# Feed-forward of a hybrid trunk: a seven-product unit in place of the second plain unit, with another order of its blocks

## Chip, cores and metric

The kernel runs on one core of a Trainium2 chip. The metric is the device time of one execution in microseconds (us), lower is better; the time before is the median of three runs, 2020.74 us (2019.19 to 2021.62).

## What is computed

A decoder trunk of four layers on 256 tokens of width 1024, in float32. Each layer is a macaron: half a gated feed-forward, a mixer (stick-breaking attention, Mamba-2 SSD, gated short convolution, attention again), half a gated feed-forward. So there are twelve phases, eight of them feed-forwards, and a last normalization. Only the feed-forward is touched by the change:

```
def rmsnorm(x, g):
    xf = x.astype(jnp.float32)
    y = xf * lax.rsqrt(jnp.mean(xf * xf, axis=-1, keepdims=True) + RMS_EPS)
    return (y * g.astype(jnp.float32)).astype(x.dtype)

def swiglu(x, w_gu, w_down):
    gate, up = jnp.split(x @ w_gu, 2, axis=-1)
    return (jax.nn.silu(gate) * up) @ w_down

for i in range(DEPTH):
    x = x + 0.5 * swiglu(rmsnorm(x, ffn1_norm[i]), ffn1_w_gu[i], ffn1_w_down[i])
    ...
    x = x + 0.5 * swiglu(rmsnorm(x, ffn2_norm[i]), ffn2_w_gu[i], ffn2_w_down[i])
```

`w_gu` is 1024 x 5632 (2816 gate columns, 2816 up columns), `w_down` is 2816 x 1024.

## The kernel before

**Blocks.** Weights stream from HBM in blocks of 128 x 2048 numbers, 1 MB each. A block is loaded by SyncE into one of six slots (three tiles `stage`, three in `arena`), split by ScalarE into a rounded high part `w_hi` (line 734), then by VectorE into the rest `w_lo` (line 1113), and multiplied by TensorE in three passes (high by high, low by high, high by low). `w_hi` and `w_lo` have three buffers each, so ScalarE may split block n only when TensorE has used block n - 3 (`block_used`), VectorE follows ScalarE (`hi_done`), and TensorE waits for VectorE (`lo_done`, `block_in`). A slot is loaded again once VectorE has finished the last split that reads it (`load`).

**Units.** The 2816 hidden columns of a feed-forward are cut into units, numbered 0 to 5 and named by a letter each in `UNITS` (line 51). A P unit has 512 columns in four plain blocks G0, G1, U0, U1 (gate and up, halves of the 1024 rows of `w_gu`). Each is multiplied with both halves of the tokens, 24 matmuls of 128x512. The H unit is half as wide (H0, H1). An S unit has 512 columns too, but cuts tokens, rows and gate/up into halves and takes seven products of half blocks instead of eight, in Strassen's manner: B11, A1, B22, A3, B21, A2, A4, of 12 matmuls each (`product`, line 1735). B blocks are loaded weights, A blocks are sums of them, made in place in the slots: A1 = B12 + B11 and A4 = B21 + the content of A2 are sums by VectorE (`weight_sum`, line 1251). A3 and A2 are made by GpSimd, which adds B22 from HBM onto a slot with an accumulating DMA of 1 MB: onto the slot of A1 once VectorE has finished the sum (line 672), and onto the slot of B11 once the split of A1 is done (line 675).

**After the products.** An S unit's seven results in PSUM are joined by three copies of ScalarE (`part`, line 823), five sums of VectorE (`part_sum`, line 1224) and two products with the silu (`hidden_summed`, line 1220). TensorE then turns the hidden values (`hidden_transpose`, line 1769, eight transposes for a unit of 512 columns), ScalarE and VectorE split them (lines 829, 1230), and the unit's down blocks D0 and D1 (`down`, 24 matmuls each, banks 0 to 3) multiply them with `w_down`. A unit's down blocks come later than the unit: `DOWNS` (line 52) says how many waiting down blocks are placed in each unit's stretch, and `ffn_order` (line 65) writes out the one order `FFN_ORDER` that all engines follow. Before the change it is (unit, block):

```
0G0 0G1 0U0 0U1 1B11 1A1 1B22 0D0 0D1 1A3 1B21 1A2 1A4 2H0 2H1 1D0 3B11 3A1 1D1 3B22 2D0
3A3 3B21 3A2 3A4 4G0 4G1 3D0 4U0 4U1 3D1 5B11 5A1 5B22 4D0 5A3 5B21 5A2 5A4 4D1 5D0 5D1
```

**The order on VectorE and ScalarE.** While TensorE has block i, VectorE first does what block i - 1 released (`released`), then the split of block i + 2, then a sum of weights if one is due. The sum for A1 is due when block i + 2 is a B11, that for A4 when it is a B21. ScalarE does the copies that block i - 1 released, then the split of block i + 2. Before the first block of a unit TensorE waits in `gate_banks_free`; after an S unit that is for its third copy and its third sum of parts, which reads bank 5. The lines are:

```
for i in range(len(FFN_ORDER)):
    if i >= 1:
        released(*FFN_ORDER[i - 1], i - 1)
    ...
        split(b0 + i + 2)
    if i + 2 < len(FFN_ORDER):
        u, name = FFN_ORDER[i + 2]
        if name == "B11":
            weight_sum(u, "A1")
        ...
        elif name == "B21":
            weight_sum(u, "A4")
```

Of the kernel before, what the change touches and what calls it, by code (L numbers as in the profile page):

```python
# [47 lines left out]
SSD_STAGE_SLOTS = 3  # L48


UNITS = "PSHSPS"
DOWNS = (0, 2, 1, 2, 2, 1)


def unit_col(u):

    return sum(256 if kind == "H" else 512 for kind in UNITS[:u])


def down_parts(u):  # L60

    return 1 if UNITS[u] == "H" else 2


def ffn_order():

    order, turned, waiting = [], {}, []
    for u, kind in enumerate(UNITS):
        own = {"P": ("G0", "G1", "U0", "U1"), "H": ("H0", "H1"),
               "S": ("B11", "A1", "B22", "A3", "B21", "A2", "A4")}[kind]  # L70
        own = [(u, name) for name in own]
        lead, head = {"P": (1, 2), "H": (1, 2), "S": (2, 3)}[kind]
        if u:
            waiting += [(u - 1, f"D{j}") for j in range(down_parts(u - 1))]
        now, waiting = waiting[:DOWNS[u]], waiting[DOWNS[u]:]
        order += own[:lead]
        if u:
            turned[u - 1] = len(order) - 1
        if kind == "S" and UNITS[u - 1] == "H":
            order += now[:1]  # L80
            now = now[1:]
        order += own[lead:head]
        if kind == "P":
            order += now[:1] + own[2:] + now[1:]
        else:
            order += now + own[head:]
    turned[u] = len(order) - 1
    return order + waiting + [(u, f"D{j}") for j in range(down_parts(u))], turned


FFN_ORDER, TURNED_AFTER = ffn_order()
N_UNITS, N_SUMS = len(UNITS), UNITS.count("S")
HOME = {"A1": "B11", "A2": "B11", "A3": "B12", "A4": "B21"}
# [13 lines left out]
def build_trunk(nc, x, ffn1_norm, ffn1_w_gu, ffn1_w_down, mix_norm, ffn2_norm, ffn2_w_gu,  # L107
# [98 lines left out]
    def block_columns(n):  # L206

        p = max(q for q in range(n_phases) if base[q] <= n)
        kind, i = PHASES[p][0], n - base[p]
        if kind == "ssd" and i == 1:  # L210
            return KD * SSD_HEADS
        return 4 * 3 * P if kind == "conv" and i < 16 else BLOCK
# [28 lines left out]
    for p, (kind, _, index) in enumerate(PHASES):  # L241
        for i in range(BLOCKS[kind]):
# [4 lines left out]
            u, name = FFN_ORDER[i]  # L247
# [9 lines left out]
    def sums_before(f, u):  # L257

        return N_SUMS * f + UNITS[:u].count("S")

    def hidden_banks_before(f, u):

        return f * sum(down_parts(v) for v in range(N_UNITS)) + sum(down_parts(v) for v in range(u))

    ctx = ExitStack()
    with ctx:
# [839 lines left out]
        def _(dve):  # L1106
            def split(n):

                if n >= total:
                    return  # L1110
                s, q, c = slot_of[n], n % SPLIT_SLOTS, block_columns(n)
                dve.wait_ge(hi_done, n + 1)
                dve.tensor_tensor(w_lo[q][:, 0:c], stage[s][:, 0:c], w_hi[q][:, 0:c].bitcast(F32),  # L1113
                                  ALU.subtract).then_inc(lo_done, 1)
# [93 lines left out]
            def ffn(p):  # L1208
# [24 lines left out]
                def weight_sum(u, name):  # L1233

                    w = lambda b: stage[home[p, u, b][0]][:, :]
                    done = len(SUM_STEP) * sums_before(f, u)
                    if name == "A1":
                        dve.wait_ge(stage_in[home[p, u, "B12"][0]], home[p, u, "B12"][1])
                        to, a, b = w("B11"), w("B12"), w("B11")
                    elif name == "A3":  # L1240
                        dve.wait_ge(stage_in[home[p, u, "B22"][0]], home[p, u, "B22"][1])
                        to, a, b = w("B12"), w("B22"), w("B12")
                    elif name == "A2":
                        to, a, b = w("B11"), w("B22"), w("B11")
                    else:
                        if BY_DMA:
                            dve.wait_ge(a2_in, 16 * (sums_before(f, u) + 1))
                        else:
                            dve.wait_ge(w_summed, done + SUM_STEP["A2"])
                        to, a, b = w("B21"), w("B21"), w("B11")  # L1250
                    dve.tensor_tensor(to, a, b, ALU.add).then_inc(w_summed, 1)

                def x_sums():
                    for i, (a, b, op) in enumerate(((xg[:, 1, :], xg[:, 3, :], ALU.subtract),
                                                    (x_sum[:, 0, :], xg[:, 0, :], ALU.subtract),
                                                    (xg[:, 0, :], xg[:, 1, :], ALU.subtract),
                                                    (xg[:, 2, :], x_sum[:, 1, :], ALU.add))):
                        if i in (1, 3):
                            dve.wait_ge(x_summed, 4 * f + i)
                        dve.tensor_tensor(x_sum[:, i, :], a, b, op).then_inc(x_summed, 1)  # L1260

                def x_sums_lo():
                    for i in range(4):
                        dve.wait_ge(xs_hi_done, 4 * f + i + 1)
                        hi, lo = sum_pair(i)
                        dve.tensor_tensor(lo, x_sum[:, i, :].rearrange("p (k t) -> p k t", k=4), hi.bitcast(F32),
                                          ALU.subtract).then_inc(xs_lo_done, 1)

                def released(u, name, i):

                    if name == "U1":
                        hidden(u, i, 512, lambda h: bank[6 + h][:, :])
                    elif name == "H1":
                        hidden(u, i, 256, lambda h: bank[4 + h][:, 256:512])
                    elif name == "A3":
                        dve.wait_ge(block_used, b0 + i + 1)
                        part_sum(u, p57, p5, bank[6][:, :], 2, ALU.subtract)
                    elif name == "B21":
                        dve.wait_ge(block_used, b0 + i + 1)
                        part_sum(u, hid[:, 0, :], bank[7][:, :], p1, 1, ALU.add)  # L1280
                    elif name == "A2":
                        part_sum(u, sg[:, 0, :], bank[5][:, :], p16, 3, ALU.subtract)
                        dve.wait_ge(part_summed, 5 * sums_before(f, u) + 1)
                        part_sum(u, sg[:, 1, :], p57, p16, 3, ALU.subtract)
                    elif name == "A4":
                        dve.wait_ge(block_used, b0 + i + 1)
                        part_sum(u, hid[:, 1, :], bank[6][:, :], p16, 3, ALU.add)
                        hidden_summed(u, 0)
                        hidden_summed(u, 1)
                        if u == N_UNITS - 1:  # L1290
                            split(b0 + i + 2)
                    for v in range(N_UNITS):
                        if TURNED_AFTER[v] == i:
                            hidden_lo(v)
                    if name == "A1" and not BY_DMA:
                        weight_sum(u, "A3")
# [4 lines that stand above are left out]
                    if i == 1 and N_SUMS:  # L1301
                        x_sums()
                    if i + 2 <= len(FFN_ORDER) and (i == 0 or FFN_ORDER[i - 1] != (N_UNITS - 1, "A2")):
                        split(b0 + i + 2)
                    if i + 2 < len(FFN_ORDER):
                        u, name = FFN_ORDER[i + 2]
                        if name == "B11":
                            weight_sum(u, "A1")
                        elif name == "A3" and not BY_DMA:
                            weight_sum(u, "A2")  # L1310
                        elif name == "B21":
                            weight_sum(u, "A4")
                    if i == 2 and N_SUMS:
                        x_sums_lo()
# [893 lines left out]
```

## Time and profile before

| | value |
|---|---|
| median of three runs | 2020.74 us |
| profiled execution, its own time | 2019.88 us |
| its span, first to last instruction | 2018.0 us |
| PE (TensorE matmul) busy | 1998.2 us, 99% |
| DVE (VectorE) busy | 1566.5 us, 78% |
| ACT (ScalarE) busy | 1187.3 us, 59% |
| POOL (GpSimd) busy | 168.7 us, 8% |
| granted TensorE clock | 1.00 throughout |
| moved by DMA | 419.87 MB, 208 GB/s in the mean |

PE is matmuls, PEld the loads of its stationary operand, which run beside them. A matmul's duration overlaps the next one's, so what it costs is the distance from start to start. The same holds for short overlaps of 0.08 us on DVE. One feed-forward, the fourth phase, lasts from 500.17 us to 678.97 us of the span: 178.80 us.

### The profile page before, as it was taken

To read this page: it belongs to the slowest core of one execution; us is meant where nothing else is said; L and a number is where in the kernel's file an instruction comes from. 1 tells how busy PE (TensorE), PEld (TensorE's weight loads), DVE (VectorE), ACT (ScalarE), POOL (GpSimd) and SP (SyncE) were. 2 spreads that over 40 slices of the span, in tenths; PEclk is the share of its full clock that TensorE was granted. 3 is DMA by queue.
4 is the path that set the end of the run, shared out by engine and by line. 5 is a ranking of instruction groups with operands and counts; after the bars stand their busy time and mean duration, and the time that the engine had idled before them with its cause. 6 is when DMAs were issued, how large, how long until landed. Compare 5 with 4: busy or idle time off the path is not lost.

```text
span 2018.0 us, 25283 instructions
## 1 busy us (share of the span) xinstructions
PE 1998.2 (99%) x10299; PEld 1705.1 (84%) x10299; DVE 1566.5 (78%) x1489; ACT 1187.3 (59%) x1269; POOL 168.7 (8%) x165
## 2 busy tenths in 40 slices
PE   7999999999999999999999999999999999999998
PEld 6888998888888899988888888988888888998887
DVE  6778567778886889968878878778878778568777
ACT  6546576556655676646556555446556556576555
POOL 2000001000000014410001000000001001001000
PEclk9999999999999999999999999999999999999999
DMA  8867535867787484368876867658876867535864
GB/s 275 257 226 229 184 105 138 252 235 229 232 248 210 139 274 132 126 229 239 242 217 194 245 241 193 206 189 248 248 219 188 253 222 232 178 105 142 256 229 114
DMA packets 242183, 419.87 MB, mean 208 GB/s; under 512 B 10668, under 2 KB 92932, under 8 KB 241556
## 3 DMA queue, kind: packets, MB, share of 16 engines
q1 hardware_dynamic: 215732, 363.34, 53.0%
q0 software_dynamic: 26048, 54.61, 15.0%
q8 instruction: 82, 1.34, 0.3%
q10 hardware_dynamic: 288, 0.31, 0.0%
q14 instruction: 33, 0.27, 0.0%
HBM read 417.14 MB, written 1.08 MB: 207 GB/s over the span
## 4 chain that ended last, share of the span: by engine, by line
PE 87%; DVE 7%; ACT 3%; issue 1%; DMA 1%; ACTq 0%; SPq 0%; POOLq 0%; POOL 0%; DVEq 0%
PE bank L1594 51%; PE bank L1735 23%; PE bank L1600 7%; DVE w_lo L1113 3%; PE bank L1769 2%; DVE arena L1461 2%; ACT w_hi L734 2%; PE bank L1627 1%; PE bank L1909 1%; PE bank L1940 1%; DMA stage<-in_ssd_w_in 0%; PE bank L1922 0%; ACT arena L1009 0%; DMA arena<-seg_rows 0%; DMA arena<-in_ffn_norm 0%
## 5 line engine op out<-in xcount | busy, mean ns | idle before, releaser
L1113 DVE TENSOR_TENSOR w_lo<-stage,w_hi 128x2048 fp32r<-128x2048 f32 (+1 forms) x224 | 514.8, 2300 | 152.4 <-ACT w_hi L734 151.2
L1113 DVE TENSOR_TENSOR w_lo<-arena,w_hi 128x2048 fp32r<-128x2048 f32 (+1 forms) x196 | 444.3, 2268 | 162.4 <-ACT w_hi L734 161.7
L734 ACT ACTIVATE w_hi<-stage 128x2048 fp32r<-128x2048 f32 (+1 forms) x224 | 423.3, 1892 | 207.5 <-PE bank L1594 141.7
L734 ACT ACTIVATE w_hi<-arena 128x2048 fp32r<-128x2048 f32 (+1 forms) x196 | 371.7, 1897 | 236.8 <-PE bank L1594 157.0
L1594 PE MATMUL bank<-w_hi,mt_hi 128*128 128x512 f32 x928 | 367.3, 396 | 0.4 <-DVE mt_lo L1347 0.4
L1594 PE MATMUL bank<-w_lo,mt_hi 128*128 128x512 f32 x928 | 361.5, 390 | 0.0
L1594 PE MATMUL bank<-w_hi,mt_lo 128*128 128x512 f32 x928 | 361.0, 390 | 0.0
L1594 PE MATMUL bank<-w_hi,xt_hi 128*128 128x512 f32 x704 | 279.2, 398 | 3.0 <-DVE w_lo L1113 1.3
L1594 PE MATMUL bank<-w_lo,xt_hi 128*128 128x512 f32 x704 | 274.8, 391 | 0.0
L1594 PE MATMUL bank<-w_hi,xt_lo 128*128 128x512 f32 x704 | 251.9, 390 | 0.0
L1594 PEld LDWEIGHTS bank<-w_hi,mt_lo 128*128 128x128 f32 x928 | 174.1, 188 | 37.0
L1600 PE MATMUL bank<-xt_hi,w_hi 128*128 128x256 f32 x704 | 203.4, 290 | 1.2 <-DVE arena L1461 0.7
L1594 PEld LDWEIGHTS bank<-w_hi,mt_hi 128*128 128x128 f32 x928 | 174.3, 188 | 35.1 <-DVE mt_lo L1347 0.8
L1594 PEld LDWEIGHTS bank<-w_lo,mt_hi 128*128 128x128 f32 x928 | 174.5, 188 | 34.5
L1600 PE MATMUL bank<-xt_hi,w_lo 128*128 128x256 f32 x704 | 198.1, 283 | 0.0
L1600 PE MATMUL bank<-xt_lo,w_hi 128*128 128x256 f32 x704 | 195.4, 283 | 0.0
L1594 PEld LDWEIGHTS bank<-w_hi,xt_hi 128*128 128x128 f32 x704 | 133.0, 189 | 33.9 <-issue 3.9
L1594 PEld LDWEIGHTS bank<-w_hi,xt_lo 128*128 128x128 f32 x704 | 132.0, 188 | 27.9
L1594 PEld LDWEIGHTS bank<-w_lo,xt_hi 128*128 128x128 f32 x704 | 133.0, 189 | 26.3
L1735 PE MATMUL bank<-w_hi,mt_hi 128*128 128x512 f32 x384 | 151.0, 393 | 0.1
L1735 PE MATMUL bank<-w_hi,mt_lo 128*128 128x512 f32 x384 | 149.7, 390 | 0.0
L1735 PE MATMUL bank<-w_lo,mt_hi 128*128 128x512 f32 x384 | 149.5, 389 | 0.0
(219 smaller groups left out, 2810.8 us busy)
## 6 DMA issues: line engine op xcount, KB each, us to landing
arena<-in_ffn_w_gu SPq DMA_DIRECT2D x81, 1024.0 KB, 5.3
stage<-in_ffn_w_gu SPq DMA_DIRECT2D x79, 1024.0 KB, 5.3
stage<-in_ffn_w_down SPq DMA_DIRECT2D x96, 512.0 KB, 5.0
arena<-in_ffn_w_down SPq DMA_DIRECT2D x80, 512.0 KB, 4.9
arena<-in_ffn_w_gu POOLq DMA_DIRECT2D x29, 1024.0 KB, 9.6
stage<-in_ffn_w_gu POOLq DMA_DIRECT2D x19, 1024.0 KB, 9.8
stage<-in_ffn_w_gu SPq DMA_DIRECT2D x18, 512.0 KB, 8.7
stage<-in_sb_w_qkv SPq DMA_DIRECT2D x16, 512.0 KB, 4.6
```

The lines of the kernel that those rows point to most:

```text
L734: act.activation(w_hi[q][:, 0:c], stage[s][:, 0:c], ACT.Copy).then_inc(hi_done, 1)
L1113: dve.tensor_tensor(w_lo[q][:, 0:c], stage[s][:, 0:c], w_hi[q][:, 0:c].bitcast(F32), ALU.subtract).then_inc(lo_done, 1)
L1461: dve.scalar_tensor_tensor(chan[:, c, i:SEQ], bank[c][:, 0:SEQ - i], par[:, t:t + 1], chan[:, c, i:SEQ], ALU.mult, ALU.add).then_inc(tap_d ...
L1594: mm = pe.matmul(out_, x_[a], w[b], start=start and (a, b) == (0, 0), stop=stop and (a, b) == (1, 0))
L1600: mm = pe.matmul(out_, w[b], x_[a], start=start and (a, b) == (0, 0), stop=stop and (a, b) == (1, 0), skip_group_check=True)
L1627: mm = pe.transpose(tb[i % 2][:, k * P:(k + 1) * P], xk, ident[:, :])
L1735: mm = pe.matmul(out_[:, :], x[a], w[b], start=start and k == 0 and (a, b) == (0, 0), stop=stop and k == 3 and (a, b) == (1, 0), skip_grou ...
L1769: mm = pe.transpose(tb[b][:, c * SEQ + h * P:c * SEQ + (h + 1) * P], hid[:, h, col:col + P], ident[:, :])
L1909: pe.matmul(z[:, 0:SEQ], kk[:, 0:P], qq, start=True, stop=True, skip_group_check=True)
L1940: pe.matmul(o[:, 0:SEQ], v(0), w[:, 0:SEQ], start=h % 2 == 0, stop=True, skip_group_check=True)
```

## The change

The letters of unit 4 become S, and three units of seven products stand behind each other (3, 4, 5). Where an S unit follows an S unit, the first down block that is placed there goes between its first product B11 and its second one A1, and VectorE's sum for A1 is due one block later (when block i + 1 is B11, not i + 2). `DOWNS` places the down blocks otherwise.

```
--- before
+++ after
@@
-UNITS = "PSHSPS"
-DOWNS = (0, 2, 1, 2, 2, 1)
+UNITS = "PSHSSS"
+DOWNS = (0, 1, 1, 2, 2, 2)
@@
+def adjacent(u):
+
+    return u > 0 and UNITS[u - 1:u + 1] == "SS"
@@ def ffn_order():
         now, waiting = waiting[:DOWNS[u]], waiting[DOWNS[u]:]
-        order += own[:lead]
+        if adjacent(u):
+            order += own[:1] + now[:1]
+            order += own[1:lead]
+            now = now[1:]
+        else:
+            order += own[:lead]
@@ VectorE, ffn(p)
+                    if i + 1 < len(FFN_ORDER):
+                        u, name = FFN_ORDER[i + 1]
+                        if name == "B11" and adjacent(u):
+                            weight_sum(u, "A1")
                     if i + 2 < len(FFN_ORDER):
                         u, name = FFN_ORDER[i + 2]
-                        if name == "B11":
+                        if name == "B11" and not adjacent(u):
                             weight_sum(u, "A1")
```

The order is now, 45 blocks in place of 42:

```
0G0 0G1 0U0 0U1 1B11 1A1 1B22 0D0 1A3 1B21 1A2 1A4 2H0 2H1 0D1 3B11 3A1 1D0 3B22 1D1
3A3 3B21 3A2 3A4 4B11 2D0 4A1 4B22 3D0 4A3 4B21 4A2 4A4 5B11 3D1 5A1 5B22 4D0 5A3 5B21 5A2 5A4 4D1 5D0 5D1
```

What moves on VectorE where unit 3 ends and unit 4 begins, in the first feed-forward. `w_lo` rows are splits, the rows arena<-...bank are sums of parts, 128x2048 rows with no `w_lo` are sums of weights; the number of a `stage` or `arena` slot differs between phases. Before:

```order
L1113 TENSOR_TENSOR w_lo0<-stage2,w_hi0 128x2048 [waits hi_done]
L1224 TENSOR_TENSOR arena<-bank7,arena 128x512 [waits part_copied,block_used]
L1113 TENSOR_TENSOR w_lo1<-arena,w_hi1 128x2048 [waits hi_done]
L1224 TENSOR_TENSOR arena<-bank5,arena 128x512 [waits part_copied]
L1224 TENSOR_TENSOR arena<-arena 128x512 [waits part_copied,part_summed]
L1113 TENSOR_TENSOR w_lo2<-stage0,w_hi2 128x2048 [waits hi_done]
L1224 TENSOR_TENSOR arena<-bank6,arena 128x512 [waits part_copied,block_used]
L1220 TENSOR_TENSOR arena<-arena 128x512 [waits part_summed,silu_done] x2
L1113 TENSOR_TENSOR w_lo0<-stage1,w_hi0 128x2048 [waits hi_done]
```

The four splits are those of 3A4, 4G0, 4G1 and 3D0. After:

```order
L1123 TENSOR_TENSOR w_lo2<-stage1,w_hi2 128x2048 [waits hi_done]
L1234 TENSOR_TENSOR arena<-bank7,arena 128x512 [waits part_copied,block_used]
L1123 TENSOR_TENSOR w_lo0<-stage2,w_hi0 128x2048 [waits hi_done]
L1234 TENSOR_TENSOR arena<-bank5,arena 128x512 [waits part_copied]
L1234 TENSOR_TENSOR arena<-arena 128x512 [waits part_copied,part_summed]
L1123 TENSOR_TENSOR w_lo1<-stage0,w_hi1 128x2048 [waits hi_done]
L1261 TENSOR_TENSOR stage2<-arena,stage2 128x2048 [waits stage_in3]
L1234 TENSOR_TENSOR arena<-bank6,arena 128x512 [waits part_copied,block_used]
L1230 TENSOR_TENSOR arena<-arena 128x512 [waits part_summed,silu_done] x2
L1123 TENSOR_TENSOR w_lo2<-stage2,w_hi2 128x2048 [waits hi_done]
```

The splits are now those of 3A4, 4B11, 2D0 and 4A1, and between that of 2D0 and the last sums of unit 3 stands the sum for 4A1, whose result the next split (of 4A1) reads. The same rows come again where unit 4 ends and unit 5 begins, with 3D1 in the place of 2D0.

On GpSimd, the accumulating transfers of the first feed-forward, before:

```order
L672 DMA arena<-in_ffn_w_gu 128x4x512 [waits w_summed]
L675 DMA arena<-in_ffn_w_gu 128x4x512 [waits lo_done]
L672 DMA arena<-in_ffn_w_gu 128x4x512 [waits w_summed]
L675 DMA arena<-in_ffn_w_gu 128x4x512 [waits lo_done]
L672 DMA stage<-in_ffn_w_gu 128x4x512 [waits w_summed]
L675 DMA arena<-in_ffn_w_gu 128x4x512 [waits lo_done]
```

and after:

```order
L682 DMA arena<-in_ffn_w_gu 128x4x512 [waits w_summed]
L685 DMA arena<-in_ffn_w_gu 128x4x512 [waits lo_done]
L682 DMA arena<-in_ffn_w_gu 128x4x512 [waits w_summed]
L685 DMA arena<-in_ffn_w_gu 128x4x512 [waits lo_done]
L682 DMA arena<-in_ffn_w_gu 128x4x512 [waits w_summed]
L685 DMA stage<-in_ffn_w_gu 128x4x512 [waits lo_done]
L682 DMA arena<-in_ffn_w_gu 128x4x512 [waits w_summed]
L685 DMA stage<-in_ffn_w_gu 128x4x512 [waits lo_done]
```

There are eight in place of six, two for each S unit.

## Rows read from the trace of the kernel before

**Rows 1.** The page: engines' busy time, and the chain that ended last.

```profile
PE 1998.2 (99%) x10299; PEld 1705.1 (84%) x10299; DVE 1566.5 (78%) x1489; ACT 1187.3 (59%) x1269; POOL 168.7 (8%) x165
...
PE 87%; DVE 7%; ACT 3%; issue 1%; DMA 1%; ACTq 0%; SPq 0%; POOLq 0%; POOL 0%; DVEq 0%
```

**Rows 2.** Timeline of PE: start us, us, what; starts of 3A3, 4G0, its turn, 4G1, 3D0.

```profile
590.37 0.39 PE L1735 MATMUL bank<-w_hi,mt_hi 128*128 128x512 f32 x1
...
601.25 0.44 PE L1594 MATMUL bank<-w_hi,xt_hi 128*128 128x512 f32 x1
...
606.75 1.04 PE L1769 MATMUL bank<-ident,arena 128*128 128x128 f32 x8
607.54 0.48 PE L1594 MATMUL bank<-w_hi,xt_hi 128*128 128x512 f32 x1
...
613.11 0.39 PE L1594 MATMUL bank<-w_hi,mt_hi 128*128 128x512 f32 x1
```

**Rows 3.** Timeline of DVE from 3A3 to the end of unit 3, [idle before <-releaser].

```profile
592.58 2.29 DVE L1113 TENSOR_TENSOR w_lo<-arena,w_hi 128x2048 fp32r<-128x2048 f32 x1 [0.94 <-ACT w_hi L734]
594.79 0.68 DVE L1224 TENSOR_TENSOR arena<-arena,bank 128x512 f32<-128x512 f32 x1
595.38 2.29 DVE L1113 TENSOR_TENSOR w_lo<-stage,w_hi 128x2048 fp32r<-128x2048 f32 x1
...
598.19 2.28 DVE L1113 TENSOR_TENSOR w_lo<-stage,w_hi 128x2048 fp32r<-128x2048 f32 x1
600.39 0.68 DVE L1224 TENSOR_TENSOR arena<-bank,arena 128x512 f32<-128x512 f32 x1
600.99 0.68 DVE L1224 TENSOR_TENSOR arena<-arena 128x512 f32<-128x512 f32 x1
601.59 2.28 DVE L1113 TENSOR_TENSOR w_lo<-stage,w_hi 128x2048 fp32r<-128x2048 f32 x1
603.79 0.68 DVE L1224 TENSOR_TENSOR arena<-bank,arena 128x512 f32<-128x512 f32 x1
604.39 1.28 DVE L1220 TENSOR_TENSOR arena<-arena 128x512 f32<-128x512 f32 x2
605.59 2.28 DVE L1113 TENSOR_TENSOR w_lo<-arena,w_hi 128x2048 fp32r<-128x2048 f32 x1
```

**Rows 4.** Timeline of ACT: the split that starts as 3A3 does.

```profile
590.63 1.92 ACT L734 ACTIVATE w_hi<-arena 128x2048 fp32r<-128x2048 f32 x1 [3.52 <-PE bank L1594]
```

**Rows 5.** Timeline around a weight sum: who starts when it ends, and the second transfer.

```profile
517.25 2.29 DVE L1251 TENSOR_TENSOR arena<-arena 128x2048 f32<-128x2048 f32 x1
519.45 2.49 DVE L1266 TENSOR_TENSOR mt_lo<-arena,mt_hi 128x512 fp32r<-128x512 f32 x4
519.57 1.92 ACT L734 ACTIVATE w_hi<-arena 128x2048 fp32r<-128x2048 f32 x1 [2.48 <-DVE arena L1251]
519.83 1.34 POOL L672 DMA_DIRECT2D arena<-in_ffn_w_gu  x1 [14.19 <-DVE arena L1251]
521.86 2.29 DVE L1113 TENSOR_TENSOR w_lo<-arena,w_hi 128x2048 fp32r<-128x2048 f32 x1
...
524.45 1.27 POOL L675 DMA_DIRECT2D arena<-in_ffn_w_gu  x1 [3.27 <-DVE w_lo L1113]
```

**Rows 6.** Timeline at the one place where PE waited for a split.

```profile
19.59 2.28 DVE L1113 TENSOR_TENSOR w_lo<-stage,w_hi 128x2048 fp32r<-128x2048 f32 x1
...
21.93 0.50 PE L1594 MATMUL bank<-w_hi,xt_hi 128*128 128x512 f32 x1 [1.28 <-DVE w_lo L1113]
...
22.26 0.40 PE L1594 MATMUL bank<-w_lo,xt_hi 128*128 128x512 f32 x1
22.26 0.19 PEld L1594 LDWEIGHTS bank<-w_hi,xt_hi 128*128 128x128 f32 x1
22.50 0.40 PE L1594 MATMUL bank<-w_hi,xt_hi 128*128 128x512 f32 x1
```

**Rows 7.** Timeline of PE: starts of 1A1 and of 0D0, with 1A1, turn, 1B22 between.

```profile
525.25 0.39 PE L1735 MATMUL bank<-w_hi,mt_hi 128*128 128x512 f32 x1
...
531.74 0.39 PE L1594 MATMUL bank<-w_hi,mt_hi 128*128 128x512 f32 x1
```

**Rows 8.** Landing times of GpSimd's transfers, line 672 and then line 675.

```profile
DMA to landing us min/median/max: 8.5/8.7/10.1
...
DMA to landing us min/median/max: 9.6/10.5/12.2
```

**Rows 9.** DMA queues from 515 to 540 us, where two accumulating transfers run.

```profile
q0 software_dynamic: 1056, 2.10, 47.8%
```

## The prediction

> **What bounds the kernel now.** I read the page first: TensorE's matmuls are busy 99% of the span and the chain that ended last is 87% PE, so a matmul saved is time saved only as long as nothing else begins to hold TensorE up [rows 1]. Then I read the timeline of one feed-forward. The four products 3A3 to 3A4 take from 590.37 to 601.25 us, 10.88 us or 2.72 us a product of 12 matmuls, with no gap [rows 2]; a plain or down block of 24 matmuls is two of those, 5.44 us. Then I asked how near the others are to holding TensorE up. In a run of products a new split is due every 2.72 us, VectorE's split costs 2.21 us from start to start (592.58 to 594.79) and a sum of parts after it 0.60 us [rows 3]: together 2.81 us, more than a product lasts. So VectorE falls behind by a little with each product there and recovers under down blocks. The reader should see in [rows 3] that only the first row has idle time ahead of it: from 592.58 to 607.87 us VectorE doesn't stop, and the change puts one more weight sum into that very stretch.
>
> **What the change saves.** In each of the eight feed-forwards unit 4 costs TensorE seven products in place of four plain blocks: 7 x 2.72 = 19.04 us for 4 x 5.44 = 21.76 us. Saved: 2.72 us each, 21.8 us in all. The down blocks are the same eleven, only elsewhere.
>
> **What it adds, beside TensorE.** Per feed-forward VectorE gets three more splits, two weight sums and five sums of parts, 3 x 2.21 + 2 x 2.20 + 5 x 0.60 = 14.0 us; ScalarE three splits and three copies, some 3 x 1.92 + 3 x 0.60 = 7.6 us; GpSimd two more accumulating transfers. By totals all this fits: VectorE would reach (1566.5 + 8 x 14.0) / 2016 = 83%. What counts is where TensorE waits for it.
>
> **The walk through a pair of seven-product units.** I set time 0 at the start of 3A3 (590.37 us). Until unit 3 ends, both orders let VectorE do the same: the split of 3A2 at 592.58, which is 2.21 (ScalarE began its part 0.26 after block 1D1 or 2D0 ended, 590.63 [rows 4], took 1.92, and VectorE followed 0.03 later), then the rows of [rows 3]. In the new order the splits that begin at 7.82 (598.19) and 11.22 (601.59) are those of 4B11 and 2D0.
> 1. 4B11 is due at 10.88. Its split ends at 10.10, but bank 5 is free only when the sum that begins at 600.39 ends, 10.70. 4G0 waits for the same sum now and starts on time, at 601.25, at the price of slower first matmuls [rows 2, 3]. No new cost.
> 2. 2D0 is due at 13.60. Its split ends at 603.87, 13.50. On time, by 0.1 us.
> 3. The weight sum for 4A1 comes where the sum of parts at 603.79 stands now, at 13.42, and lasts 2.29: until 15.71. ScalarE splits 4A1 only then. After such a sum it starts 0.03 later (519.54 to 519.57, [rows 5]), so from 15.74 to 17.66. VectorE has meanwhile done the last three small operations of unit 3 (3 x 0.60 from 15.63, until 17.4) and splits from 17.69 to 19.98.
> 4. 4A1 is due at 13.60 + 5.44 = 19.04. In the one place where TensorE waits for a split now, it starts 0.06 after it ended (21.87 to 21.93), and the next two matmuls come 0.33 and 0.24 later in place of 0.227 each, 0.12 lost [rows 6]. So 4A1 is worth a start at 19.98 + 0.18 = 20.16. **Lost: 1.12 us**, with whatever 4B11 and 2D0 lost inside it, since 19.98 is set by VectorE alone. The down block in between is what keeps it from being 6.6 us.
> 5. The turn of unit 3's hidden values. Now it stands inside 4G0 and 4G1, 11.86 us from 601.25 to 613.11 [rows 2] for 10.88 of matmuls: 0.98 beside them. After an A1, 1A1 and 1B22 take from 525.25 to 531.74 [rows 7], 6.49 for 5.44: 1.05. New cost 0.07.
> 6. Then: 4A1 ends at 22.88, 4B22 at 26.65, 3D0 at 32.09, where 4A3 starts. The two accumulating transfers are issued 0.29 and 0.30 after what they wait for [rows 5], at 16.00 and 20.28. The first lands after 8.7 us in the median [rows 8], 24.7, about when ScalarE turns to 4A3. The second lands after 10.5, at 30.8. VectorE has finished the splits of 4A3 and 4B21 at about 31.1, so the sum for 4A4 runs from there to 33.3, and the split of 4A2, which ScalarE can start at 32.35, begins on VectorE at 34.30: 2.21 after 4A3, just as at 592.58. No cost, and the pattern starts afresh.
> 7. Unit 4 into unit 5: the same walk, 1.12 us. The turn after 5A1 is there already.
> 8. Unit 1 has one down block before 1A3 in place of two. That is unit 5's present form (5B22 4D0 5A3), which runs without a gap. Its accumulating transfers start at 519.83 and 524.45 [rows 5], land at 534 or so (at 536.7 for the longest, 12.2), and the split of 1A2 would begin at 539.4 (0D0, from 531.74 [rows 7] to 537.18, and 2.21). Costed at nothing; its cover is 0D0.
>
> **Sum.** Per feed-forward -2.72 + 2 x 1.12 + 0.07 = -0.41 us; times eight, **-3.3 us**. The profiled execution took 2019.88 us, its span 2018.0; the change would bring it to 2016.6. The median of the runs, 2020.74, is 0.9 above it: 2017.4. This is 0.16% less, within the 0.2% (4 us) that a measurement of this kernel can tell from no change.
>
> **Bounds.** The price that no row shows in place is the restart. If 4A1 started the moment its split ended and lost nothing, the loss would be 0.94 and the total -6.2 (2014.5). If 2D0 or the sum cost 0.2 us more than in the walk (the late 2D0 has only 0.1 to spare), it would be 1.32 and the total -0.1 (2020.6). I take 1.12, since [rows 6] show the same wait on the same engine. To be faster by over 4.04 us the loss would have to be below 1.08, so the call is close.
>
> **Transfers under a busy VectorE.** GpSimd's transfer at 519.83 was issued and done with in 1.34 us while VectorE ran without a stop from 519.45 to 524.1 [rows 5]; the walk takes this for granted at 16.00 and 20.28. The Trainium skill, "SBUF — State Buffer", summary of rules for kernel authors, advises against hiding a GpSimd-issued transfer under VectorE, because descriptors starve while VectorE is in its two-port modes; its section on who interferes with whom excepts tensor_tensor, with the reason marked as inferred. By the exception the sum stays; by the bare rule it would be the last rival below. The trace agrees with the exception.
>
> **The rivals.**
> (a) *The second pair inherits a delay.* If the first transfer takes its longest time, 10.1, ScalarE's split of 4A3 starts at 26.1 and VectorE's run ends 0.4 later; if the second takes 12.2, it lands at 32.5 and the sum for 4A4 ends 0.4 too late. Both are seen [rows 8]; the medians speak against them. 0.4 x 8 = 3.2 us: 2020.6.
> (b) *Slower: the accumulating transfers of unit 4 land late.* From 11.8 us after issue on (32.1) each further microsecond of the second one delays the sum for 4A4, the split of 4A2 and all that VectorE does until 5A1, so it costs 8 us in all. For it: two such transfers take the 16 DMA engines 0.478 x 25 = 12.0 us [rows 9], and units 4 and 5 now ask for them within some 32 us beside six blocks of plain loads. Against: there too, plain loads ran beside them. At 13.3 us: 1.5 x 8 = +12, so 2029.
> (c) *The wait at 4A1 doesn't come*, because the sum is ready sooner than in the walk; then the saving stays but for the turns: 2020.74 - 21.8 + 0.6 = 1999.5. If one of the two pairs is free of it, 2008.5. Against it: VectorE's rows leave no room before 15.71.
> (d) *Descriptors wait for VectorE.* The first transfer would be issued at the next idle time, 17.4 in place of 16.00, and land at 26.1: as (a) in its price, 0.4 x 8, 2020.6. The rule stands in the paragraph on transfers; [rows 5] speak against it.
>
> **How the numbers follow.** The walk: 0.66, of it 0.29 below 2016.7 and 0.37 above, since the loss need differ by only 0.04. (a) 0.13, nearly all within no change. (b) 0.10, slower. (c) 0.09, faster. (d) 0.02, no change. Faster 0.38, no change 0.51, slower 0.11. The predicted time is the walk's, 2017.4. The range goes from 2013.5 (the walk's lower bound with a microsecond for the measurement) to 2023.5 (the walk with (a), and the mild end of (b)).
>
> **What would show it.** In the new profile TensorE waits for VectorE's split once at 4A1 and once at 5A1, 16 times, with about 0.9 us idle each (some 15 us; there is 1.3 now), 4A1 starting 20.04 after 3A3 and 4A3 32.1 after it; a feed-forward lasts 178.4 us in place of 178.80. PE's busy time falls by about 18 to 20 us while the span hardly moves. VectorE shows the sum at 13.42 and the split of 4A1 at 17.69. Wrong would be: no wait at the A1 blocks, waits at 4A2 or 5A2 or for a transfer, or a gap before 1A3 or 1A2.

## The result, and the profile after

The changed kernel takes **2039.36 us** in the median of 4 runs (2038.14 to 2041.04); the kernel before took 2020.01 beside it (4 runs, 2019.19 to 2021.62). The ratio is 1.0095, with a 95% interval of 1.0078 to 1.0113: slower by 19 us, where 2017.4 and no measurable change were forecast. The prediction was wrong. What came is the mechanism of rival (b), late landings, in unit 5 more than in unit 4.

The page of the profiled execution (2038.14 us, span 2036.4), engines' busy time and then the chain that ended last:

```profile
PE 1991.5 (98%) x10203; PEld 1682.1 (83%) x10203; DVE 1676.0 (82%) x1569; ACT 1244.2 (61%) x1317; POOL 189.2 (9%) x181
...
PE 59%; DVE 20%; DMA 12%; ACT 5%; issue 4%; ACTq 0%; SPq 0%; POOLq 0%; DVEq 0%; POOL 0%
```

Against [rows 1]: TensorE is busy 6.7 us less, as 96 matmuls are gone, but the span is 18.4 longer, so it stands idle 25.1 us more. The chain has lost 28 points of PE; DVE has 20% in place of 7, and **DMA 12% in place of 1**. That last figure is the lead: before, transfers were hardly on the path that sets the end.

The waits of TensorE, the groups on VectorE's results (engine, line, waited for: us in total, times, longest):

```profile
PE bank L1749 <- DVE w_lo L1123: 22.9, 24, 2.0
...
PE bank L1749 <- DVE arena L1234: 2.1, 5, 0.5
PE bank L1608 <- DVE w_lo L1123: 1.3, 1, 1.3
```

Sixteen waits for a split were forecast, two a feed-forward; there are 24 on line 1749. The five for `arena L1234` are at 5B11, for a sum of unit 4's parts. The timeline of PE in the third feed-forward (the fourth phase), whose 3A3 starts at 588.47, names the third:

```profile
588.47 0.39 PE L1749 MATMUL bank<-w_hi,mt_hi 128*128 128x512 f32 x1
...
608.51 0.50 PE L1749 MATMUL bank<-w_hi,mt_hi 128*128 128x512 f32 x1 [0.72 <-DVE w_lo L1123]
...
620.60 0.39 PE L1749 MATMUL bank<-w_hi,mt_hi 128*128 128x512 f32 x1
...
640.85 0.50 PE L1749 MATMUL bank<-w_hi,mt_hi 128*128 128x512 f32 x1 [0.72 <-DVE w_lo L1123]
...
659.84 0.50 PE L1749 MATMUL bank<-w_hi,mt_hi 128*128 128x512 f32 x1 [1.29 <-DVE w_lo L1123]
```

These are 3A3, 4A1, 4A3, 5A1 and, new, **5A2**, which starts 1.45 us late. What it waited for is read one engine back at a time. The timelines of POOL, ACT and DVE around it (GpSimd's second accumulating transfer of unit 5, then ScalarE's split of what it brings, then the weight sum for 5A4 and VectorE's split of 5A2):

```profile
641.09 1.28 POOL L685 DMA_DIRECT2D stage<-in_ffn_w_gu  x1 [3.00 <-DVE w_lo L1123]
...
655.29 1.92 ACT L744 ACTIVATE w_hi<-stage 128x2048 fp32r<-128x2048 f32 x1 [5.61 <-DMA stage<-in_ffn_w_gu]
...
655.29 2.29 DVE L1261 TENSOR_TENSOR arena<-arena,stage 128x2048 f32<-128x2048 f32 x1 [3.18 <-DMA stage<-in_ffn_w_gu]
657.50 2.28 DVE L1123 TENSOR_TENSOR w_lo<-stage,w_hi 128x2048 fp32r<-128x2048 f32 x1
```

The transfer is issued at 641.09 and lands 14.2 us later. ScalarE had been idle for 5.61 us and VectorE for 3.18, both with nothing but this transfer to wait for. From the landing, a sum and a split end at 659.78, and TensorE starts 0.06 later. So a transfer, not an engine, sets 5A2. The landings of GpSimd's lines, first and second transfer (672 and 675 before):

```profile
DMA to landing us min/median/max: 8.5/8.7/9.6
...
DMA to landing us min/median/max: 9.5/11.8/14.9
```

The first is as in [rows 8]; the second has gone from a median of 10.5 to 11.8 and from a longest of 12.2 to 14.9. By units, over the eight feed-forwards: unit 4's took 11.8 to 13.0, unit 5's 13.8 to 14.9. With 5A2 due at 658.39, 1.45 before 659.84, a landing of unit 5's up to 12.7 us after issue costs nothing.

Why they are slow stands in the DMA view from 634 to 659 us (40 slices of 0.625 us; 16 engines; then the queues):

```profile
DMA  0057999698999999999999999999999999999950
GB/s 0 0 131 223 419 426 406 108 79 108 190 206 203 197 193 210 210 167 177 275 282 301 301 282 308 305 288 288 295 315 295 305 338 423 387 410 413 413 190 26
...
q0 software_dynamic: 1056, 2.10, 49.4%
q1 hardware_dynamic: 1391, 4.19, 44.2%
```

The engines are 90% busy or more in all but a few slices. Plain loads alone reach 406 to 426 GB/s, an accumulating transfer alone only 190 to 210; where both run, from slice 20 on, they share. SyncE issues the loads of 5D0 and 5D1 (2 MB) at 643.1 and 645.3, just behind the transfer that TensorE will need first, and one of the next phase (1 MB) at 649.9.

How much of the plain loads moved beside a second transfer, from its issue to its landing, is in the DMA view of just that stretch. These are the lines for unit 5 before (635.27 to 646.53, landed after 11.3 us), and for unit 4 (608.75 to 620.80, 12.1) and unit 5 (641.09 to 655.27, 14.2) of the changed kernel:

```profile
q1 hardware_dynamic: 248, 0.95, 21.5%
...
q1 hardware_dynamic: 541, 1.13, 27.3%
...
q1 hardware_dynamic: 542, 2.01, 37.5%
```

More plain data beside it goes with a later landing.

### The profile page after: what moved, and what is told of

Same layout as the page of the kernel before. It is cut to its first block, busy times and chain, and to the rows that moved or that the text cites. A ratio compares the mean times of both kernels' runs of the same rounds, so it can differ in the third digit from the quotient of the medians.

```text
span 2036.4 us, 25299 instructions
## 1 busy us (share of the span) xinstructions
PE 1991.5 (98%) x10203; PEld 1682.1 (83%) x10203; DVE 1676.0 (82%) x1569; ACT 1244.2 (61%) x1317; POOL 189.2 (9%) x181
## 4 chain that ended last, share of the span: by engine, by line
PE 59%; DVE 20%; DMA 12%; ACT 5%; issue 4%; ACTq 0%; SPq 0%; POOLq 0%; DVEq 0%; POOL 0%
PE bank L1608 34%; PE bank L1749 13%; DVE w_lo L1123 11%; PE bank L1614 7%; DMA stage<-in_ffn_w_gu 5%; DMA arena<-in_ffn_w_gu 5%; ACT w_hi L744 4%; DVE arena L1261 2%; DVE arena L1475 2%; DVE arena L1234 2%; DVE stage L1261 1%; PE bank L1783 1%; PE bank L1641 1%; PE bank L1923 1%; PE bank L1954 1%
## 5 line engine op out<-in xcount | busy, mean ns | idle before, releaser
L1123 DVE TENSOR_TENSOR w_lo<-stage,w_hi 128x2048 fp32r<-128x2048 f32 (+1 forms) x232 | 532.8, 2300 | 96.1 <-ACT w_hi L744 94.9
L744 ACT ACTIVATE w_hi<-stage 128x2048 fp32r<-128x2048 f32 (+1 forms) x232 | 438.5, 1892 | 214.7 <-PE bank L1608 92.6
L1123 DVE TENSOR_TENSOR w_lo<-arena,w_hi 128x2048 fp32r<-128x2048 f32 (+1 forms) x212 | 480.4, 2269 | 89.7 <-ACT w_hi L744 89.3
L744 ACT ACTIVATE w_hi<-arena 128x2048 fp32r<-128x2048 f32 (+1 forms) x212 | 402.0, 1898 | 207.2 <-PE bank L1608 85.9
L1608 PE MATMUL bank<-w_hi,mt_hi 128*128 128x512 f32 x928 | 368.0, 397 | 0.4 <-DVE mt_lo L1361 0.4
L1608 PE MATMUL bank<-w_lo,mt_hi 128*128 128x512 f32 x928 | 361.6, 390 | 0.0
L1608 PE MATMUL bank<-w_hi,mt_lo 128*128 128x512 f32 x928 | 361.1, 390 | 0.0
L1749 PE MATMUL bank<-w_hi,mt_hi 128*128 128x512 f32 x512 | 204.7, 400 | 23.2 <-DVE w_lo L1123 22.9
L1749 PE MATMUL bank<-w_hi,mt_lo 128*128 128x512 f32 x512 | 199.9, 390 | 0.0
L1749 PE MATMUL bank<-w_lo,mt_hi 128*128 128x512 f32 x512 | 199.6, 390 | 0.0
L1608 PE MATMUL bank<-w_hi,xt_hi 128*128 128x512 f32 x448 | 178.6, 400 | 3.0 <-DVE w_lo L1123 1.3
L1608 PE MATMUL bank<-w_lo,xt_hi 128*128 128x512 f32 x448 | 175.4, 393 | 0.0
L1749 PE MATMUL bank<-w_hi,xt_hi 128*128 128x512 f32 x384 | 151.2, 394 | 2.1 <-DVE arena L1234 2.1
L1608 PE MATMUL bank<-w_hi,xt_lo 128*128 128x512 f32 x448 | 152.0, 390 | 0.0
L1749 PE MATMUL bank<-w_hi,xt_lo 128*128 128x512 f32 x384 | 149.7, 390 | 0.0
L1749 PE MATMUL bank<-w_lo,xt_hi 128*128 128x512 f32 x384 | 149.5, 389 | 0.0
```

The lines of the kernel that those rows point to most:

```text
L744: act.activation(w_hi[q][:, 0:c], stage[s][:, 0:c], ACT.Copy).then_inc(hi_done, 1)
L1608: mm = pe.matmul(out_, x_[a], w[b], start=start and (a, b) == (0, 0), stop=stop and (a, b) == (1, 0))
L1749: mm = pe.matmul(out_[:, :], x[a], w[b], start=start and k == 0 and (a, b) == (0, 0), stop=stop and k == 3 and (a, b) == (1, 0), skip_grou ...
```

## The experiments

Times before, run beside them: 2020.35 for the first four (25 runs), 2020.05 for the next four (8 runs), 2020.36 for the last two (15 runs). Intervals are 95% intervals of the ratio to it.

**k1: the second transfers of units 4 and 5 made short**, a quarter of their data. Are they the cause at all?

```diff
-                    pool.dma_start(stage[to][:, :].rearrange("p (k c) -> p k c", k=4), b22,
+                    ks = slice(0, 1) if adjacent(u) else slice(0, 4)
+                    pool.dma_start(stage[to][:, :].rearrange("p (k c) -> p k c", k=4)[:, ks, :], b22[:, ks, :],
```

> The changed kernel, but the second accumulating transfer of units 4 and 5 (line 685) adds only the first 512 columns of the slot, 256 KB in place of 1 MB, so three quarters of B22 are missing from A2 and A4 of these units. Theory L (landing): what lies beyond the forecast comes from this transfer landing 12 to 15 us after its issue, which holds the sum for 4A4 and 5A4 and the split of 5A2. Then landings fall to under 9 us, TensorE's waits at 5A2 go, those at 4A1 and 5A1 (0.9 us each) stay, and the time falls by some 2.2 us a feed-forward, to 2021. Theory V (VectorE): its queue in units 4 and 5 is full whatever the transfers do; then the waits at 5A2 stay and the time stays at 2039.

Measured: 2016.82 us, 0.9981 [0.9972, 0.9991]; these transfers land after 5.8 to 7.8 us. The waits:

```profile
PE bank L1750 <- DVE w_lo L1124: 11.7, 16, 0.8
...
PE bank L1609 <- DVE w_lo L1124: 1.3, 1, 1.3
```

Sixteen waits, at 4A1 and 5A1, and 22.5 us less than the changed kernel: with the late landing the whole loss is gone, and what is left is the time forecast (2017.4), below the 2021 that I gave this run. The run also moves fewer bytes, so it doesn't tell a late landing from busy DMA engines in general.

**k2: the weight sums of 4A1 and 5A1 on 8 of 2048 columns**, to price the waits at A1.

```diff
+                    if name == "A1" and adjacent(u):
+                        dve.wait_ge(lo_done, base[p] + FFN_ORDER.index((u, "B11")) + 1)
+                        to, a, b = to[:, 0:8], a[:, 0:8], b[:, 0:8]
```

> The changed kernel, but VectorE's weight sum for 4A1 and 5A1 is done on 8 of 2048 columns (A1 of these units is otherwise B11 alone). Both theories: the splits of 4A1 and 5A1 end 2.2 us earlier, and TensorE's waits there go (2 x 1.1 us a feed-forward). Theory L: the second transfer is issued 2.2 us earlier while TensorE comes 1.1 us earlier at each pair, so the wait at 5A2 shrinks from about 1.5 to about 0.5: 2039 - 8 x 3.6 = 2010. Theory V: 14 us less work for VectorE in the full stretch, nothing is late any more: 2000.

Measured: 2071.96 us, 1.0253 [1.0236, 1.0269], 33 us slower than the changed kernel though it does less: both expectations missed, in sign too. 4A1 and 5A1 waited no more; 4A2 and 5A2 waited instead. The waits:

```profile
PE bank L1752 <- DVE w_lo L1123: 46.7, 16, 4.7
```

The landings of the two transfers:

```profile
DMA to landing us min/median/max: 8.5/9.9/12.9
...
DMA to landing us min/median/max: 9.6/13.5/18.6
```

Both of GpSimd's transfers are now slow. In the third feed-forward, SyncE had issued a plain load at 613.27, 0.34 us before GpSimd's first at 613.61, which landed after 11.5; it issued the next at 619.91, and the second transfer, of 617.89, landed after 15.6. It looks as if the loads that run beside the transfers decide, and as if an earlier VectorE had moved those loads too; this run doesn't show it by itself, and k7 tests it.

**k3: the units of before with the new places of the down blocks.**

```diff
-UNITS = "PSHSSS"
+UNITS = "PSHSPS"
```

> The units of before (unit 4 plain again) with the new places of the down blocks alone. Theory L and V: no seven-product unit stands behind another, no block is late; 2020, as before. Rival: the new places of the down blocks, one before 1A3 in place of two, cost time by themselves; then 2022 or more.

Measured: 2020.02 us, 0.9997 [0.9988, 1.0007]. The places of the down blocks cost nothing by themselves.

**k4: one plain load held back.** The computation is complete, and so is every transfer.

```diff
+                if (u, name) == (N_UNITS - 1, "D0"):
+                    sp.wait_ge(a2_in, 16 * (sums_before(nth("ffn", p), u) + 1))
```

> The changed kernel, but SyncE issues the load of 5D0 (and all after it) only when the second accumulating transfer of unit 5 has landed, so that the loads of 5D0, 5D1 and of the next phase do not run beside it. Theory L, with the plain loads as the reason for the late landing: the landing of unit 5 falls from 14 to 11 us, the wait at 5A2 goes, 2039 - 8 x 1.7 = 2025. If the landing is late for another reason than the plain loads beside it, it stays at 14 and the time at 2039. Theory V: 2039 too. If the held loads are then late themselves, a wait shows at 5D0 or at the start of the next phase.

Measured: 2020.34 us, 1.0001 [0.9992, 1.0011]. One wait that holds the load of 5D0 and those behind it until unit 5's second transfer has landed takes back 19 us, more than I expected. That transfer lands after 9.1 to 10.7 us, unit 4's still after 11.9 to 12.9. The DMA view from 628 to 653 us shows the loads standing behind it, from the slice with 52 on:

```profile
DMA  5000937998959999999999999999202989999999
GB/s 210 3 0 0 111 72 308 419 419 328 92 69 141 203 210 210 203 210 206 200 187 206 210 206 210 210 206 177 46 0 52 105 321 419 419 419 406 419 419 400
```

No byte less is moved, so it is the moment of the loads that costs the time, not their sum.

**k5: the waits at A1 by themselves**, with the whole computation: sum and split of 4A1 and 5A1 in two halves, so that ScalarE splits the first while VectorE sums the second.

```diff
+                        for k, semaphore in enumerate((half_sum, w_summed)):
+                            w = slice(1024 * k, 1024 * (k + 1))
...
+                            dve.tensor_tensor(to[:, w], a[:, w], b[:, w], ALU.add).then_inc(semaphore, 1)
...
+                    act.wait_ge(half_sum, halved(n))
+                    act.activation(w_hi[q][:, 0:1024], stage[s][:, 0:1024], ACT.Copy).then_inc(half_hi, 1)
+                    act.wait_ge(w_summed, len(SUM_STEP) * sums + SUM_STEP[name])
+                    act.activation(w_hi[q][:, 1024:2048], stage[s][:, 1024:2048], ACT.Copy).then_inc(hi_done, 1)
```

VectorE's split of A1 is halved likewise and stands ahead of the last small operations of the unit before.

> The changed kernel, with the weight sum and the split of 4A1 and 5A1 in two halves of 1024 columns, so that ScalarE can start on the first half when half the sum is there, and with VectorE's split of them ahead of the two products with the silu. Theory L (the transfers' landing, lengthened by plain loads beside them) with the walk of the prediction for the rest: the splits of 4A1 and 5A1 end at 18.7 after 3A3 in place of 19.98, before the block is due at 19.04, so both waits of 1.1 us go. The second transfer is issued 1.3 us earlier and TensorE comes 1.1 earlier, so the wait at 5A2 (1.5 us) stays or shrinks little: 2039 - 8 x 2.3 = 2020. If the waits at the A1 blocks come from something else than this chain, nothing moves: 2039.

Measured: 2037.91 us (2032.07 to 2042.99), 1.0086 [1.0065, 1.0107]: missed. In the third feed-forward the waits at A1 are gone (ahead of 4A1 0.03 us are lost in place of 0.91), but nothing came of it. The timelines of POOL and PE there, the second transfer of unit 5 and then 5A2:

```profile
635.61 1.28 POOL L697 DMA_DIRECT2D stage<-in_ffn_w_gu  x1 [1.59 <-DVE w_lo L1145]
...
655.25 0.50 PE L1784 MATMUL bank<-w_hi,mt_hi 128*128 128x512 f32 x1 [1.90 <-DVE w_lo L1149]
```

The transfer is issued 2.87 us after the first in place of 4.27, and lands after 15.1 in place of 14.2. Issued earlier is not landed earlier: what TensorE gained at 5A1 it gave back at 5A2.

**k6: k5 with the hold of k4.**

> k5_halved and k4_hold together: halves, and SyncE's load of 5D0 held until the second transfer of unit 5 has landed. Theory L with the walk: all three waits of a feed-forward go, and what is left is the saved product less 0.1 us of turn: 2020.3 - 8 x 2.5 = 2000. If VectorE's full queue is a limit of its own (13 us more work a feed-forward), waits show up elsewhere, at the A2 and A4 blocks of unit 4 and 5, and the time is above 2006.

Measured: 2013.04 us, 0.9966 [0.9953, 0.9979]. Better by 25 us than k5, but short of what was expected: unit 4's second transfer, which nothing protects, lands after 12.8 to 14.0, and 4B21, 4A2 and 4A4 together lose 0.9 to 1.9 us a feed-forward, 10.7 in all.

**k7: k2 with two holds**, one for each unit, on the load of 5B11 and on that of 4D1.

```diff
+                if (u, name) == (5, "B11"):
+                    sp.wait_ge(a2_in, 16 * (sums_before(nth("ffn", p), 4) + 1))
+                if (u, name) == (4, "D1"):
+                    sp.wait_ge(a2_in, 16 * (sums_before(nth("ffn", p), 5) + 1))
```

> k2_tiny_sum (sum for 4A1 and 5A1 on 8 columns) with two holds: SyncE loads 5B11 and all after it only when unit 4's second transfer has landed, and 4D1 and all after it only when unit 5's has. In k2 the first transfers landed after 12 us and the second ones after 16 to 18. Theory L: that was because 5B11 (and 4D1) were now loaded in the same instant, a full megabyte ahead of or beside them; with the holds the landings are back at 9 and 10 us and the time falls from 2072 to about 2001. If the lengthening has another cause (the transfers' own early start), the landings stay above 12 and the time above 2040.

Measured: 2000.10 us, 0.99 [0.9885, 0.9915], as expected: 72 us from two waits on SyncE. In units 4 and 5 the first transfers land after 8.6 to 10.0 us and the second ones after 9.1 to 10.5, and no feed-forward has a wait of TensorE for a split of a seven-product unit. With nothing lost, the change is worth the 20 us of its arithmetic.

**k8: k5 with the two holds**, the whole computation.

> k5_halved with the two holds of k7: no plain load runs beside unit 4's and unit 5's transfers. Theory L with the walk: as k6 or slightly better, 1999 to 2002, the landings of unit 4 at 9.5 in place of 12. If the held loads (5B11, 5B12, 3D1, 5B22) then come late themselves, waits for a DMA show at 3D1 or at the sum for 5A1, and it is slower than k6.

Measured: 2007.41 us, 0.9931 [0.9915, 0.9948], 5 us above the range. The second transfers land after 10.9 to 11.5 us in unit 4 and 10.5 to 11.9 in unit 5, early enough, but 3D1 now waits. The waits:

```profile
PE bank L1647 <- DVE w_lo L1153: 6.1, 7, 1.9
```

One of the seven, of 1.3 us, was there before; the other six are at 3D1, 4.8 us together. The timeline at 3D1 of the third feed-forward, of ACT and of PE:

```profile
623.01 1.92 ACT L767 ACTIVATE w_hi<-arena 128x2048 fp32r<-128x2048 f32 x1 [1.66 <-DMA arena<-in_ffn_w_down]
...
627.31 0.50 PE L1647 MATMUL bank<-w_hi,mt_hi 128*128 128x512 f32 x1 [1.10 <-DVE w_lo L1153]
```

The held load of 5B11 starts at 611.28, those of 5B12 and 3D1 queue behind it, and 3D1's lands only at 623.0. So the hold was probably one load too early, which k10 tests.

**k9: the changed kernel with the two holds and nothing else.** This is the test of the prediction's walk with its failed assumption mended.

> The changed kernel with nothing but the two holds of the eighth run: the load of 5B11 waits until unit 4's second accumulating transfer has landed, the load of 4D1 until unit 5's has. The computation is complete. Theory L (only late landings separate the changed kernel from the walk): both second transfers land 9 to 11 us after issue, TensorE waits at 4A1 and 5A1 as in the walk (1.1 us each) and nowhere else in the feed-forwards, and the time is 2016 to 2019 us, some 20 us under the changed kernel. Rival H (what is held comes late): the plain loads behind the held one are late instead, as 3D1 is in the eighth run, at 1 to 2 us a feed-forward: 2022 to 2032 us. Rival V (VectorE's load, not the landings, makes the loss): 2035 to 2040 us, as the changed kernel.

Measured: **2017.69 us**, 0.9987 [0.9978, 0.9995]. The waits:

```profile
PE bank L1753 <- DVE w_lo L1127: 11.7, 16, 0.8
```

4A1 and 5A1 in the timeline of PE (3A3 starts at 584.62, so 4A1 is at 20.05):

```profile
604.67 0.50 PE L1753 MATMUL bank<-w_hi,mt_hi 128*128 128x512 f32 x1 [0.75 <-DVE w_lo L1127]
...
637.01 0.50 PE L1753 MATMUL bank<-w_hi,mt_hi 128*128 128x512 f32 x1 [0.72 <-DVE w_lo L1127]
```

Theory L holds; rival V falls, and rival H as the larger cause. VectorE's work and the bytes are as in the changed kernel; only the moment of the held loads and of those queued behind them differs, and 22 us go with it. The second transfers land after 9.0 to 11.0 us. Part of rival H is true, though small: in the third feed-forward 5B11 and 3D1 take 0.22 us longer than in the changed kernel.

**k10: k8 with its first hold on 5B12**, one load later.

> The eighth run with its first hold one load later: the load of 5B12, not that of 5B11, waits for unit 4's second transfer. Complete computation. If 3D1 waits in the eighth run because the held loads start too late, the wait (6.1 us in all) goes with it: 2000 to 2003 us. Against it, the load of 5B11 now runs beside unit 4's transfers, as in the run with halves and one hold, where they took 12.8 to 14.0 us: then 4A2 waits again, up to 1 us a feed-forward, and the time is 2008 to 2013 us.

Measured: **2002.39 us**, 0.9912 [0.9899, 0.9926], with the whole computation. The waits:

```profile
PE bank L1647 <- DVE w_lo L1153: 1.3, 1, 1.3
...
PE bank L1788 <- DVE w_lo L1153: 0.6, 1, 0.6
```

The first of them is the one in the first feed-forward that was there before; the second is at 4A2 of the last feed-forward. The load of 5B11 is out before unit 4's transfers this time and does them little harm (it was issued at 593.56, and GpSimd's first transfer at 596.10; second landings 10.5 to 12.4). This version beats the kernel before by 18 us and the changed one by 37.

## Why the prediction was wrong

Point by point, with times after 3A3 in the third feed-forward:

- **The saving** was right: seven products last 7 x 2.72, and k7 has it all and k10 nearly (2000.1 and 2002.4; rival (c) put a kernel without the waits at 1999.5).
- **Points 1 to 4 were right**, the three times that count to 0.01 us. The weight sum begins at 13.42, the split of 4A1 at 17.69, 4A1 at 20.04, as forecast. Of the wait only 0.72 us shows as idle time, as the walk's 0.06 and 0.12 lie in the restart and 2D0 before it was itself 0.08 late.
- **Point 5** was right: from 4B11 to 4B22 the four blocks take 0.08, 0.91, 1.10 and 0.12 us more than their matmuls, 2.21 in all, for a wait of 1.12 and a turn of 1.05.
- **Point 6 failed**: "The second lands after 10.5, at 30.8. ... No cost, and the pattern starts afresh." Issued at 20.28 as forecast, it landed after 12.1 in unit 4. That is the step that failed: the walk put both second landings at the median of [rows 8], 10.5 us, and over the eight feed-forwards they took 11.8 to 13.0 in unit 4 and 13.8 to 14.9 in unit 5. In unit 4 here 4A3 came at 32.13 for 32.09 and 4A2 on time with 0.73 to spare, but 4A4 lost 0.18, as 5B11 waits for VectorE. That median was taken over units that differ: unit 5 before already had the slowest landings of the three, 10.7 to 12.2 with a median of 11.3.
- **Point 7 failed the same way, and here it decided**: "the same walk, 1.12 us". Unit 5 meets the loads of 5D0 and 5D1 as well, and lands after 14.2. Of the third feed-forward, k9 lasts 171.96 us from its first block to 5D1 and the changed kernel 173.88; 1.45 of these 1.92 are the wait at 5A2, 0.23 the slower blocks right behind it, 0.26 what 4D1 loses more and 0.18 what 4A4 loses; against it stand the 0.22 that the holds cost k9. Over all eight feed-forwards, 4B21, 4A2 and 4A4 lose 4.3 us in the changed kernel and nothing in k9, 5B21, 5A2 and 5A4 14.3 and nothing, and 4D1 loses 2.2 more; k9's holds cost 0.4. That is 20.4; the spans of the two, 2036.4 and 2016.3, differ by 20.1.
- **Point 8** was right: 1A3 and 1A2 wait for nothing.
- **The sum**: -3.3 forecast; k9, where the landings are what point 6 took them to be, gives 2017.69 less 2020.36, -2.7. The bounds were drawn around a wait that was already right, while the term that varied had a row with 9.6 to 12.2 in it and entered the walk as one number, its longest value only as rival (a).
- **Rival (b)** had the right mechanism and 0.10. Its evidence, 12.0 us of all 16 DMA engines for two transfers [rows 9], was the stronger: in k4's view, with no plain load beside them, they keep the engines 90% busy or more at some 206 GB/s, so plain loads beside them must delay them. I let "there too, plain loads ran beside them" outweigh it without counting them. The count: 1.13 MB moved beside unit 4's transfer and 2.01 MB beside unit 5's, and none in k9, where the same two landed after 9.5 and 9.6. That is 2.2 and 2.3 us for each MB, near the 2.4 that a MB takes at 410 GB/s. The price was right for unit 4: in each of the eight feed-forwards, what 4B21, 4A2 and 4A4 lose together is the landing, counted from 3A3, less 32.1 us (32.10 to 32.15). It left out unit 5, where only a landing after 12.7 us costs, since no unit follows; its landings were later than that by more, and 14.3 of the 20 us lie there.
- **Rival (d)** fell. GpSimd's first transfer is issued at 16.00, 0.30 after the sum, while VectorE runs on. This is the timeline of POOL at that place:

```profile
604.47 1.27 POOL L682 DMA_DIRECT2D arena<-in_ffn_w_gu  x1 [33.44 <-DVE stage L1261]
608.75 1.27 POOL L685 DMA_DIRECT2D stage<-in_ffn_w_gu  x1 [3.00 <-DVE w_lo L1123]
```

The second is issued at 20.28, as in the walk, under a split. The Trainium skill, "SBUF — State Buffer", on who interferes with whom, excepts tensor_tensor from the rule that VectorE keeps GpSimd's descriptors waiting; the trace agrees with the exception, 1.27 us an issue here too. By the bare rule of that page's summary the issues would have been late, and they weren't: the time was lost behind the issue, on the DMA engines.

- **What would show it**: the waits at 4A1 and 5A1 and the two starts on VectorE came as written; "waits at 4A2 or 5A2 or for a transfer" was the sign of being wrong, and came too. PE's busy time fell by 6.7 us in the changed kernel where 18 to 20 were forecast, since only part of a loss shows as idle time (1.29 of the 1.68 us round 5A2), and by 18.7 in k10 (to 1979.5), where almost nothing holds it up.

What stays open: how the DMA engines divide themselves between the queues was seen only in its result, so the 2.2 to 2.4 us a MB are what these runs gave, not a rule. The profiled runs of k10 and k7 differ by 1.8 us of span, and 1.6 of it lie in the last feed-forward of k10, where unit 4's second transfer took 12.4 us; why that one was slow with no plain load in its flight stays open.

## What to carry to other kernels

A landing time is not a property of a transfer: before it enters a walk, list the plain loads that the new order issues between its issue and its due time. Their bytes at the plain rate, added to the landing with none beside it, are an upper estimate: beside unit 4's and unit 5's transfer SyncE issued 3 MB each, of which 1.13 and 2.01 MB moved before the landing. Where a slow transfer is on the path, hold the loads that are needed later until it has landed, but hold none that must itself arrive soon (k8 against k10). Here two waits on the issuing engine were worth 22 us, and only with such waits did the halved sum pay: 1.5 us without them, less than k5's own spread (k5 against the changed kernel), and 15.3 with them (k10 against k9). When removing a wait makes a kernel slower, look at what its earlier finish has moved on the queues.

## What the runs showed of the hardware

An accumulating transfer from HBM costs the DMA engines about twice what a plain load does: from 634 to 659 us 2.10 MB took 49.4% of 25 us of all 16 engines, 5.9 us a MB, and 4.19 MB of plain loads 44.2%, 2.6 us a MB. Alone the one runs at some 206 GB/s and the other at some 410.

Whether a transfer is slow depends on small shifts: GpSimd's first transfer landed after 8.8 us in the changed kernel, with a plain load of 1 MB issued 2.47 us before it (602.00 and 604.47), and after 11.5 in k2, with one issued 0.34 us before it.

In k2 TensorE's clock fell behind a long wait. The mean granted clock of that run is 0.991, against 0.999 here, and the table by 1 us stretches (us, PE busy, granted clock, DMA share, GB/s) shows where, at 5A2 of the third feed-forward, which starts at 674.65 after 4.42 us of idle time:

```profile
673.00:674.00 1.00, 0.00 (x0) 1.00 0.03 8
674.00:675.00 1.00, 0.35 (x1) 0.72 0.00 0
675.00:676.00 1.00, 1.00 (x3) 0.50 0.22 35
676.00:677.00 1.00, 1.00 (x4) 0.50 0.62 96
677.00:678.00 1.00, 1.00 (x4) 0.57 0.00 0
678.00:679.00 1.00, 1.00 (x6) 1.00 0.00 0
```

For some 3 us it is at 0.50, the lower level of 1.2 GHz, and a row counts 3 or 4 matmuls that touch it in place of 6. The wait of 1.29 us at 5A2 in the changed kernel had no such fall behind it: the granted clock from 660 to 670 us was 1.00. So this wait cost k2 about 1.5 us more than its length, an estimate: half of those 3 us.
